# The end of a two-block model on one core: last hidden block transposed earlier, last down unit by column halves, last combination added onto the transposed x

## The reference, cut to what matters

```python
def moe_swiglu(h, w_router, w_gate, w_up, w_down):      # top 2 of 8 experts, width 3584
    ...
    def expert_block(args):
        xb, e = args
        return (jax.nn.silu(xb @ w_gate[e]) * (xb @ w_up[e])) @ w_down[e]
    ...
    y = ybuf[dest] * gates.reshape(m)[order][:, None].astype(ybuf.dtype)
    out = jnp.zeros_like(hf).at[tok].add(y)
...
x = x + moe_swiglu(h, moe_router[j], moe_w_gate[j], moe_w_up[j], moe_w_down[j])
return rmsnorm(x, norm_final)      # x * rsqrt(mean(x*x) + 1e-5) * w
```

## Time and profile before

| | |
|---|---|
| median of three runs | 2175.09 us |
| span of the profiled execution, first to last instruction | 2172.6 us |
| TensorE busy | 2135.3 us |
| mean granted TensorE clock | 0.993 |
| from the first transposition of the last hidden block to the end | 22.3 us |

### The profile page before, as it was taken

One profiled execution on the slowest core, in us unless ns is written; L12 is line 12 of the kernel. 1 busy time (PEld: TensorE's weight loads), 2 busy tenths in 40 slices (PEclk: granted clock), 3 DMA queues, 4 the chain that ended last, 5 costly groups with the idle time before them and its releaser, 6 DMA issues.

```text
span 2172.6 us, 33531 instructions
## 1 busy us (share of the span) xinstructions
PE 2135.3 (98%) x13316; PEld 1901.5 (88%) x13316; DVE 1417.4 (65%) x1420; ACT 1290.4 (59%) x1404; POOL 655.1 (30%) x318
## 2 busy tenths in 40 slices
PE   9999999999999999999999999999999999999998
PEld 8979999988999898999997888888888888888886
DVE  1455223336422784222775989999999989899996
ACT  4546445455644534444534777777777777777775
POOL 6717885726787103888201000000000000000000
PEclk9999999999999999999998999999999999999999
DMA  7434554525455334555444999999999999999994
GB/s 239 135 98 153 174 194 144 180 63 166 156 189 175 118 98 155 183 185 188 134 146 133 378 372 346 363 352 375 359 347 371 361 375 345 362 350 373 365 370 171
DMA packets 307360, 529.03 MB, mean 244 GB/s; under 512 B 11827, under 2 KB 152787, under 8 KB 307249
## 3 DMA queue, kind: packets, MB, share of 16 engines
q1 hardware_dynamic: 306512, 526.44, 69.5%
q0 software_dynamic: 736, 1.00, 0.2%
HBM read 525.84 MB, written 1.05 MB: 243 GB/s over the span
## 4 chain that ended last, share of the span: by engine, by line
PE 86%; POOL 5%; DVE 4%; ACT 2%; issue 2%; DMA 0%; POOLq 0%; DVEq 0%; ACTq 0%
PE bank L698 84%; POOL weights_low L2790 5%; PE bank L1365 1%; DVE qb L2098 1%; ACT sc L1476 1%; DVE sc L2098 1%; PE bank L866 0%; DVE sc L2106 0%; DVE h L2106 0%; PE bank L769 0%; ACT weights_high L1479 0%; DVE nmax L2133 0%; ACT sq L1476 0%; DVE y L2106 0%; PE bank L1271 0%
## 5 line engine op out<-in xcount | busy, mean ns | idle before, releaser
L2098 DVE TENSOR_TENSOR expert_weights_low<-ring_experts,expert_weights_high 128x2048 fp32r<-128x2048 f32 x336 | 764.8, 2288 | 79.4 <-ACT expert_weights_high L1479 79.2
L1479 ACT ACTIVATE expert_weights_high<-ring_experts 128x2048 fp32r<-128x2048 f32 x336 | 643.6, 1916 | 167.7 <-PE bank L698 167.7
L2790 POOL TENSOR_TENSOR weights_low<-ring,weights_high 128x1024 fp32r<-128x1024 f32 x254 | 620.8, 2466 | 375.0 <-ACT weights_high L1479 374.8
L1479 ACT ACTIVATE weights_high<-ring 128x1024 fp32r<-128x1024 f32 x294 | 303.6, 1056 | 341.4 <-PE bank L698 306.6
L698 PE MATMUL bank<-x_high,weights_high 128*128 128x256 f32 x1024 | 288.7, 285 | 0.8 <-POOL weights_low L2790 0.8
L698 PE MATMUL bank<-x_high,weights_low 128*128 128x256 f32 x1024 | 282.7, 279 | 0.0
L698 PE MATMUL bank<-x_low,weights_high 128*128 128x256 f32 x1024 | 280.1, 283 | 0.0
L698 PE MATMUL bank<-h_high,weights_high 128*128 128x256 f32 x704 | 199.8, 286 | 5.0 <-ACT h_high L1479 5.0
L698 PE MATMUL bank<-h_high,weights_low 128*128 128x256 f32 x704 | 198.5, 284 | 0.0
L698 PEld LDWEIGHTS bank<-x_high,weights_low 128*128 128x128 f32 x1024 | 194.3, 190 | 0.1
L698 PEld LDWEIGHTS bank<-x_high,weights_high 128*128 128x128 f32 x1024 | 192.3, 188 | 2.3 <-DVE zs L2106 1.2
(11 more groups left out here) (313 smaller groups left out, 3866.3 us busy)
## 6 DMA issues: line engine op xcount, KB each, us to landing
ring_experts<-in_moe_w_gate_dram SPq DMA_DIRECT2D x112, 1024.0 KB, 7.0
ring_experts<-in_moe_w_up_dram SPq DMA_DIRECT2D x112, 1024.0 KB, 6.6
ring_experts<-in_moe_w_down_dram SPq DMA_DIRECT2D x112, 1024.0 KB, 6.3
ring<-in_w_in_dram SPq DMA_DIRECT2D x62, 1024.0 KB, 5.3
ring<-in_w_merge_dram SPq DMA_DIRECT2D x24, 1024.0 KB, 5.1
ring<-in_w_out_dram SPq DMA_DIRECT2D x14, 1024.0 KB, 5.2
ring<-in_ffn_w_gate_dram SPq DMA_DIRECT2D x11, 1024.0 KB, 5.3
ring<-in_ffn_w_up_dram SPq DMA_DIRECT2D x11, 1024.0 KB, 5.4
```

What stands on the lines that cost most here:

```text
L1479: return nc.scalar.activation(dst, src, ACT.Copy, scale=scale)
L2098: return nc.vector.tensor_tensor(dst, x, z, op)
L2790: nc.gpsimd.tensor_tensor(half_of(wlo[:, q_slot, :], t, width), half_of(ring[:, slot, :], t, width), half_of(whi[:, q_slot, :], t, width). ...
```

## The change

TensorE gets the last loop round of the last turn written out (units 34 to 39), so that the last hidden block is transposed in the middle of unit 39, before `turn_places`; its high and low parts go into a free piece of the gathered tokens (`end_turned`), because unit 39 still reads the old one. VectorE multiplies gate and up ahead of the low part of unit 40, and writes the low part of the turned block ahead of that of unit 41. Unit 41 runs column half by column half, and `result` starts with the first half. At the end `finish` is gone: `xT` without the last expert is transposed into the banks 0, 6, 1 and 7 first, and the last combination is added onto it there by eight matmuls of 512 columns (the transposition starts the accumulation). VectorE multiplies by the norm's weights as soon as the squares are read, then applies the scale in place to three pieces, ScalarE to the fourth. The loops of OVER rounds stay where they are on every engine, and TensorE's body in them grows by the written-out round.

```diff
+X_BANKS = (0, 6, 1, 7)
+def end_turned(buf):
+    return tuple(w[1 - buf][:, 0:2, :].rearrange("p a (c n) -> p (a c) n", n=P) for w in (xgh, xgl))
+out_last = signal("last_out_row_ready")
+half_down, weighted = signal("last_down_first_half"), signal("result_weighted")
@@ SyncE, the four stores of the output
-    sp.wait_ge(out_full.h, n + 1)
+    if n < 3:
+        sp.wait_ge(out_full.h, n + 1)
+    else:
+        sp.wait_ge(out_last.h, 1)
@@ TensorE
+def down_across(turn, m, half, between, s=0):
+    wh, wl = (w[:, m % SPLITS_E, :].rearrange("p (k n) -> p k n", n=D) for w in (ewh, ewl))
+    pe.wait_ge(eh_done.h, turn * UNITS_E + s * 6 + (m + 1))
+    for kk in range(2):
+        for n in range(2):
+            cols = slice(n * 512, n * 512 + 512)
+            mm(bank[3 + n][:, :], hdTh[:, 2 * half + kk, :], wh[:, kk, cols], False, False, share=True)
+            mm(bank[3 + n][:, :], hdTl[:, 2 * half + kk, :], wh[:, kk, cols], False, False, share=True)
+    between()
+    pe.wait_ge(el_done.h, turn * UNITS_E + s * 6 + (m + 1))
+    for kk in range(2):
+        for n in range(2):
+            ins = mm(bank[3 + n][:, :], hdTh[:, 2 * half + kk, :], wl[:, kk, n * 512:n * 512 + 512],
+                     False, False, share=True)
+    ins.then_inc(e_used.h, 1)
+def down_end(turn, m, half, turned, by_columns):
+    th, tl = turned
+    wh, wl = (w[:, m % SPLITS_E, :].rearrange("p (k n) -> p k n", n=D) for w in (ewh, ewl))
+    pe.wait_ge(eh_done.h, turn * UNITS_E + (m + 1))
+    if not by_columns:
+        for kk in range(2):
+            for n in range(2):
...
+        return
+    for n in range(2):
+        cols = slice(n * 512, n * 512 + 512)
+        for kk in range(2):
+            mm(bank[3 + n][:, :], th[:, 2 * half + kk, :], wh[:, kk, cols], False, False, share=True)
+            mm(bank[3 + n][:, :], tl[:, 2 * half + kk, :], wh[:, kk, cols], False, False, share=True)
+        if n == 0:
+            pe.wait_ge(el_done.h, turn * UNITS_E + (m + 1))
+        for kk in range(2):
+            ins = mm(bank[3 + n][:, :], th[:, 2 * half + kk, :], wl[:, kk, cols], False, False, share=True)
+        ins.then_inc((half_down if n == 0 else e_used).h, 1)
-    with pe.Fori(0 if ahead is None else 1, HS - 2) as s:
+    with pe.Fori(0 if ahead is None else 1, HS - 2 if following is not None else HS - 3) as s:
-    if before is not None:
-        pe.wait_ge(comb.h, comb.at(before, 4))
-    turn_places(turn, pair, *side)
+        if before is not None:
+            pe.wait_ge(comb.h, comb.at(before, 4))
+        turn_places(turn, pair, *side)
-        turn_hidden(turn, HS - 1)
+        pe.wait_ge(mo_g.h, turn * HS + HS - 1)
+        project_e(turn, 34, 0, 0, side)
+        turn_hidden(turn, HS - 2)
+        project_e(turn, 35, 1, 0, side)
+        project_e(turn, 36, 0, 1, side)
+        pe.wait_ge(hT_ready.h, turn * HS + HS - 1)
+        down_e(turn, 37, 1)
+        project_e(turn, 38, 1, 1, side)
+        down_across(turn, 39, 0, lambda: turn_hidden(turn, HS - 1))
+        if before is not None:
+            pe.wait_ge(comb.h, comb.at(before, 4))
+        turn_places(turn, pair, *side)
-        down_e(turn, 40, 1)
-        down_e(turn, 41, 0)
+        down_end(turn, 40, 1, end_turned(side[0]), False)
+        down_end(turn, 41, 0, end_turned(side[0]), True)
-finish(n_over + (EXPERTS - 1))
+last_turn = n_over + (EXPERTS - 1)
+pe.wait_ge(comb.h, comb.at(last_turn, 0))
-    pe.wait_ge(comb.h, comb.at(n_over + (EXPERTS - 1), 2 * half + 2))
-            ins = pe.transpose(bank[1 + 2 * half + t][:, kk * P:(kk + 1) * P],
-                               xT[:, 4 * half + kk, t * P:(t + 1) * P], ident)
-        ins.then_inc(fin_full.h, 1)
+            pe.matmul(bank[X_BANKS[2 * half + t]][:, kk * P:(kk + 1) * P],
+                      xT[:, 4 * half + kk, t * P:(t + 1) * P], ident, start=kk == 0, stop=False,
+                      is_transpose=True, skip_group_check=True)
+pe.wait_ge(put_ready.h, put_ready.at(last_turn, 1))
+for half in range(2):
+    pe.wait_ge(ye_done.h, ye_done.at(last_turn, half + 1))
+    for t in range(TT):
+        b = X_BANKS[2 * half + t]
+        mm(bank[b][:, :], put[:, t * P:(t + 1) * P], yeh[:, half * 512:half * 512 + 512], False, False,
+           share=True)
+        mm(bank[b][:, :], put[:, t * P:(t + 1) * P], yel[half][:, :], False, True, share=True).then_inc(
+            fin_full.h, 1)
@@ ScalarE
-def turned(turn, q):
+def turned(turn, q, to=hdTh[:, :, :]):
-    copy(hdTh[:, :, :], views(2, 4)).then_inc(hT_high.h, 1)
-def result(turn, m):
-    unit_used(act, turn, m)
+    copy(to, views(2, 4)).then_inc(hT_high.h, 1)
+def result(turn, m, ends=None):
+        if ends is not None and n == 0:
+            act.wait_ge(half_down.h, ends)
+        else:
+            unit_used(act, turn, m)
+        turned(turn, HS - 1, end_turned(buf)[0])
-        turned(turn, HS - 1)
-        result(k + (EXPERTS - 1), UNITS_E - 1)
+        result(k + (EXPERTS - 1), UNITS_E - 1, k + 1)
-result(n_over + (EXPERTS - 1), UNITS_E - 1)
+result(n_over + (EXPERTS - 1), UNITS_E - 1, n_over + 1)
-    fn(sq[:, 2 * n:2 * n + 2, :], views(1 + n), ACT.Square, accum_out=lsum[:, 3 * t + to:3 * t + to + 1]).then_inc(
+    fn(sq[:, 2 * n:2 * n + 2, :], views(X_BANKS[n]), ACT.Square, accum_out=lsum[:, 3 * t + to:3 * t + to + 1]).then_inc(
+act.wait_ge(last_std.h, TT)
+act.wait_ge(weighted.h, 4)
+fn(h[:, 6:8, :], h[:, 6:8, :], ACT.Copy, scale=lsum[:, 3:4]).then_inc(out_last.h, 1)
@@ VectorE
-def turned_low(turn, q):
+def turned_low(turn, q, to=(hdTh[:, :, :], hdTl[:, :, :])):
-    tt_(hdTl[:, :, :], views(2, 4), hdTh[:, :, :].bitcast(F32), ALU.subtract).then_inc(hT_ready.h, 1)
+    tt_(to[1], views(2, 4), to[0].bitcast(F32), ALU.subtract).then_inc(hT_ready.h, 1)
+        times_up(turn, HS - 1, 38)
-        times_up(turn, HS - 1, 38)
+        turned_low(turn, HS - 1, end_turned(buf))
-        turned_low(turn, HS - 1)
-finish(n_over + (EXPERTS - 1))
-for t in range(TT):
-    dve.wait_ge(last_std.h, t + 1)
-    for half in range(2):
+for half in range(2):
+    for t in range(TT):
-        stt(h[:, 2 * n:2 * n + 2, :].rearrange("p a s -> p (a s)"), bank[1 + 2 * half + t][:, :], lsum[:, 3 * t:3 * t + 1],
-            wlast[:, half * 512:half * 512 + 512], ALU.mult, ALU.mult).then_inc(out_full.h, 1)
+        dve.wait_ge(last_sum.h, 2 * half + t + 1)
+        tt_(h[:, 2 * n:2 * n + 2, :].rearrange("p a s -> p (a s)"), bank[X_BANKS[2 * half + t]][:, :],
+            wlast[:, half * 512:half * 512 + 512], ALU.mult).then_inc(weighted.h, 1)
+dve.wait_ge(weighted.h, 4)
+for n in range(3):
+    dve.wait_ge(last_std.h, n // 2 + 1)
+    part = h[:, 2 * n:2 * n + 2, :].rearrange("p a s -> p (a s)")
+    ts(part, part, lsum[:, 3 * (n // 2):3 * (n // 2) + 1]).then_inc(out_full.h, 1)
```

More of the change, by code:

```diff
@@ new lines, in down_end @@
+            def down_end(turn, m, half, turned, by_columns):
[11 more added lines that the diff above has]
+                        for n in range(2):
+                            ins = mm(bank[3 + n][:, :], th[:, 2 * half + kk, :], wl[:, kk, n * 512:n * 512 + 512],
+                                     False, False, share=True)
+                    ins.then_inc(e_used.h, 1)
+                    return
+                for n in range(2):
+                    cols = slice(n * 512, n * 512 + 512)
+                    for kk in range(2):
+                        mm(bank[3 + n][:, :], th[:, 2 * half + kk, :], wh[:, kk, cols], False, False, share=True)
+                        mm(bank[3 + n][:, :], tl[:, 2 * half + kk, :], wh[:, kk, cols], False, False, share=True)
+                    if n == 0:
+                        pe.wait_ge(el_done.h, turn * UNITS_E + (m + 1))
+                    for kk in range(2):
+                        ins = mm(bank[3 + n][:, :], th[:, 2 * half + kk, :], wl[:, kk, cols], False, False, share=True)
+                    ins.then_inc((half_down if n == 0 else e_used).h, 1)
@@ L2020, in middle_step, with expert @@
                     high(turn, m, s)
-            def expert(turn, half, before=None, last=False, ahead=None):
+            def expert(turn, half, before=None, last=False, ahead=None, buf=0):
                 if before is not None:
@@ L2057, in _ @@
                 expert(e, e % 2, e - 1 if e else None, e + 1 == EXPERTS,
-                       e // 2 + 1 if e % 2 and e + 1 < EXPERTS else None)
+                       e // 2 + 1 if e % 2 and e + 1 < EXPERTS else None, (e // 2) % 2)
             with act.Fori(0, OVER) as k:
                 with act.If(n_over > k):
-                    result(k + (EXPERTS - 1), UNITS_E - 1)
+                    result(k + (EXPERTS - 1), UNITS_E - 1, k + 1)
                     for m in range(3):
@@ L2668, in middle_step, with expert @@
                 low(turn, 18, s)
-            def expert(turn, before=None, last=False, ahead=None):
+            def expert(turn, before=None, last=False, ahead=None, buf=0):
                 if before is not None:
@@ L2743, in _ @@
```

(3 more changed lines are left out.)

## The result

| | median | runs | range |
|---|---|---|---|
| before | 2173.97 us | 5 | 2171.41 to 2176.50 |
| after | 2180.86 us | 5 | 2178.97 to 2183.09 |

The ratio is 1.0035 [1.0024, 1.0046]: the change makes the kernel 6.9 us slower. I forecast 2174.1 us and gave "slower" a chance of 0.06; the range ended at 2177.4. With five runs the median of before is 2173.97, so the 2175.09 that I started from was 1.1 us high. The profiled execution has a span of 2177.9 us against 2172.6.

A forecast was written before the change was run, and what follows sets the result against it. The bound was taken to be TensorE, with a relay of waits at the end that could move. First square 3.03 us earlier, first store 1.04 later, clock fall 1.0: net 1.0, from 2175.1 to 2174.1 us; range 2171.0 to 2177.4.

The forecast's parts named there:

- slower: Outcome class for the whole kernel: a time above 2179.4 us, nearly all from repeated fetches; chance 0.06.
- Last hidden block: Last turn: `hd` moves ahead, unit 40 starts 1.44 us earlier, and TensorE's wait of 1.4 us is gone.
- Result by column halves: After unit 41: first half ready 1.4 us earlier, both done by about 2158.2, a gain only if nothing else is later.
- What is late next, the branch: TensorE's loop over unused turns: still 5.4 us, out at 2158.5, leaving 2.15 us idle before the `xT` transpositions.
- The slower rival: TensorE's loop: rounds two and three also fetch, 3.13 us more each; 5.3 us slower, 2180.4 us; chance 0.07.
- Clock: TensorE after the new idle: granted clock falls, costing 1.0 us (bounds 0 and 1.6); fall 0.47, without 0.28 (2173.1 us).
- net gain 1.0: Whole kernel: 2.0 us gained without clock effects, less 1.0 for the clock's fall, giving 2174.1 us.
- Norm and stores: The end: first store 2.01 us after the fourth square begins, 1.04 us later relative to the square than before.
- Do the quicker scalings make it good? No: Stores at the end: quicker scalings don't recover the later first store, since the end follows the first issue, not the last.
- Fetch hidden: Rival at TensorE's loop: branches cost 50 to 69 ns, TensorE isn't held up; gain 4.3 us, 2170.8 us; chance 0.11.
- Before's slow stretch: Rival: before seldom had its slow clock stretch at 2153, so the profile flatters the change by up to 1.6 us.
- the correction I kept ready: For a seldom slow stretch in before: medians equal or 0.6 us the other way, 2175.7 us.

The follow-up runs named there:

- after_head_moved: The changed kernel with its starting fillers rewritten as 74 matmuls of 152 columns, moving the loop head from offset 16 to 120; 2174.81 us, ratio 1.0001.
- head_at_64: The changed kernel with its starting fillers rewritten as 46 matmuls of 244 columns, putting the loop head at offset 64; 2172.64 us, ratio 0.9989.
- head_at_232: The changed kernel with its starting fillers rewritten as 130 matmuls of 88 columns, putting the loop head at offset 232; 2173.82 us, ratio 1.0001.
- after_no_skip: The changed kernel with TensorE's loop over the unused overflow turns left out; 2171.22 us, ratio to before 0.9988.
- before_no_skip: The kernel before with TensorE's loop over the unused overflow turns left out; 2173.62 us, ratio 0.9998.
- before_long_body: The kernel before with 80 never-run matmuls of zeros added to TensorE's overflow body (756 instructions), loop head unmoved; 2174.30 us, ratio 0.9996.
- before_head_moved: The kernel before with only its starting fillers rewritten as 98 matmuls of 116 columns, moving the loop head to offset 16; 2175.67 us, ratio 1.0004.
- tail_only: The kernel before with only the change's new end behind the overflow loop, the last turn kept in its old order; 2173.49 us, ratio 0.9994.

## Why the prediction was wrong

*Last hidden block: right.* By the common scale, `hd` was due at 0.26 and came at 0.27; its transposition at 1.81 and 1.82; unit 40 at 3.92 and 3.83; the low part of unit 41 ended at 6.05 forecast, 5.98 measured. The wait of 1.4 us and the lower clock at 2153 are gone.

*Result by column halves: right.* Both halves were due at 11.24 and were done at 11.08.

*What is late next, the branch: this step failed.* "The code between is the same, 5.4 us, so it comes out at 2158.5." Place and start were right (6.14 forecast, the loop is taken up at 6.05 to 6.24), and so was the first jump, 3.757 for 3.354 us. But the same code lies 152 instructions further on, and the second jump took 6.315 us instead of 0.221, with three more transfers on the instruction queue. The forecast carried the price of all six branches over from one layout and had no term for that. The loop took 11.9 us from its first jump to its end, and the idle was 8.75 us and not 2.15. Where the head is moved back to its old offset, the loop's first jump to its end takes 5.23 us, the idle is 2.05, and the first square comes 3.11 us earlier than in before, for 3.03 forecast.

*The slower rival came nearest.* It said that at another address a later jump would fetch again. Its time, 2180.4 us, was right by luck: it counted two more misses of 3.13, and it was one of 6.315. It also named the longer body, which the runs rule out as the condition, and head and landing place driving one another out, which no run shows. The chance of 0.07 was too small: I let two cheap jumps of one layout speak for another layout.

*Clock: a coin that fell both ways.* With an idle of 2.05 us the clock stayed at 1.00 in after_head_moved and head_at_64; in head_at_232, at 2.06, it fell. Its row and stretch:

```profile
2157.73 2.79 PE L1536 MATMUL bank<-cst,xT 128*128 128x128 f32 x16 [2.06 <-issue]
```
```profile
2159.20:2162.60 3.40, 3.40 (x13) 2.92 (x13) 0.39 (x1) 1.15 (x4) 0.00 (x0) 0.52 0.00 0
```

The fall cost 1.2 us (24.69 against 23.49), for 1.0 forecast: head_at_232 ends 0.95 us before the old kernel (24.69 for 25.64), my "net gain 1.0". The onset, 1.5 us after work resumed, was also as forecast. In after the idle of 8.75 us put the clock at 0.50 through all transpositions. Of the 11.04 us between after and after_no_skip at the first square, the transpositions start 8.91 later, and the remaining 2.13 is work at the lower clock (3.67 for 1.91, the combination 0.43 apart).

*Norm and stores: right in after.* First store 1.95 us after the fourth square, forecast 2.01; the scaling is 0.43 us, taken at 0.48. "Do the quicker scalings make it good? No" held for the forecast sum: from first store to end 4.49 us, as before (4.51). That the end follows the first issue alone is weaker: going back to one scale brought the store 0.97 forward and the end only 0.58 in the one profile, and the medians tell nothing apart.

*Fetch hidden.* The rival's 4.3 us is what the change is worth without the jumps: 4.36 by the scale (25.64 to 21.28), and 4.40 with the end written twice. The medians are 3.2 and 4.0 us below those of before. From there: a first miss costs 2.2 (23.49), a fall of the clock 1.2, the second miss and its clock the rest, to 32.28.

*Before's slow stretch.* After the same wait of 1.41 us the lower clock stood in before_no_skip's profile as well, 3.4 us from 2153.0, and in those of before_long_body and before_head_moved; in tail_only's, where that order of work is kept, the clock stayed at 1.00 from 2150 to 2165. That is four profiles of five. The medians of before (2173.97 to 2174.92 in five comparisons) do not ask for the correction I kept ready.

## What stays open

Why the second jump costs more than a first one (6.3 to 7.1 us against 3.3 to 3.9), and why offset 16 has it in only some of the executions, isn't shown. In each of the five profiles with a long second jump the back jump ahead of it took 0.45 us, otherwise 0.24, so the head itself seems to be late; that is argued, not shown. In these five the instruction queue also starts a further transfer 0.6 to 0.7 us after the start of the last one of the first jump; it takes 2.0 to 2.2 us, and two more follow, 3.0 to 3.8 us apart; in the others none follows. Which code each transfer brings, the trace doesn't say. Offsets other than 16, 64, 120 and 232 weren't tried. Two of 124 runs of before and one of head_at_232 also lie above 2179 us; there is no profile of such a run, so whether they are second misses too is open.

## What to carry to other kernels

A loop whose body is never run was not free on TensorE: its sequencer took 5.2 us to get past three rounds of it, 11.9 us with the second miss, and whatever stands behind has to wait for that. Look at the branch rows of the sequencer before removing a wait that hides them; then write the usual case so that it runs straight on (here 2170.4 us, 0.9981 [0.9972, 0.9991]) or put one condition around the whole loop. A change that moves code can cost by place alone (the profiled run of before_head_moved ends 7.07 us later than before by the scale), so rule that out by shifting the code without changing it.

## What the runs showed of the hardware

- The first far jump on TensorE (over 596 to 883 instructions) took 3.3 to 3.9 us in every profile that has one, with two or three transfers of instructions in that stretch; the second one of the same loop took 0.22 us, or 6.3 to 7.1 us with four or five transfers in all. On ScalarE and VectorE the branches over their bodies took 50 to 69 ns.
- Which of the two followed the offset of the loop's head in stretches of 256 instructions (five of six profiles at 16, none of six at 64, 120 and 232); the length of the code jumped over did not decide it (596 with and 756 without).
- After the same idle of 2.05 us the granted clock of TensorE fell to its lower level (1.2 GHz) in one profile of three.
